# A two-layer hybrid trunk: layer 0's shift and scale loaded ahead of its gate, with scale and gate multiplied on VectorE

## What is computed

```python
def _rmsnorm(x, g):
    y = x * lax.rsqrt(jnp.mean(x * x, axis=-1, keepdims=True) + EPS)
    return y * g

# for each layer l, with c (latent) and c_ctx (context)
mod_x = silu(c) @ w_ada[l] + b_ada[l]          # 3 * 1024 columns
mod_c = silu(c_ctx) @ w_ada[l] + b_ada[l]
shift_x, scale_x, gate_x = split(mod_x, 3)     # the same for mod_c

hx = _rmsnorm(x, g_pre) * (1.0 + scale_x) + shift_x
hc = _rmsnorm(xc, g_pre) * (1.0 + scale_c) + shift_c
px, pc = hx @ w_in, hc @ w_in                  # all branches' inputs
...
total = sum(sigmoid(merge_i) * ((y_i * silu(z_i)) @ w_o[i]) for i in range(4))
x_new = x + gate_x * _rmsnorm(total @ w_out, g_post)
```

## Time and profile before

| | us |
|---|---|
| median of 3 runs | 2555.64 |
| lowest and highest | 2554.72, 2561.79 |
| profiled execution, its own time | 2555.41 |
| its span in the profile | 2553.4 |
| TensorE busy / DVE / ScalarE / GpSimd | 2465.6 / 1203.7 / 1091.7 / 1155.9 |

### The profile page before, as it was taken

How to read it: one execution, slowest core, us unless ns; L and a number is a source line. 1 busy time by engine, 2 the same in 40 slices (tenths; PEclk the granted TensorE clock), 3 DMA queues, 4 the chain that set the end, 5 groups by cost and what they waited for, 6 DMA issues and landing times.

```text
span 2553.4 us, 38113 instructions
## 1 busy us (share of the span) xinstructions
PE 2465.6 (97%) x12969; PEld 2082.7 (82%) x12969; DVE 1203.7 (47%) x1788; ACT 1091.7 (43%) x2287; POOL 1155.9 (45%) x948
## 2 busy tenths in 40 slices
PE   7897999999999999999999999999999999999998
PEld 1887988799888888888888788898888788888887
DVE  2453657496254466644243465781635333333322
ACT  2645564396212443344433443892214433343333
POOL 1576993123222355555555442222223555555553
PEclk9899999999999999999999999999999999999999
DMA  6355762100121155535333531001211333344333
GB/s 255 88 143 165 220 194 78 38 2 19 49 62 36 47 173 165 177 115 174 111 108 108 172 93 49 6 1 49 64 38 36 108 111 111 111 150 134 111 111 132
DMA packets 393275, 262.40 MB, mean 103 GB/s; under 512 B 16934, under 2 KB 365750, under 8 KB 391610
## 3 DMA queue, kind: packets, MB, share of 16 engines
q1 hardware_dynamic: 378944, 227.07, 29.8%
q10 hardware_dynamic: 14204, 33.67, 3.7%
HBM read 251.23 MB, written 9.45 MB: 102 GB/s over the span
## 4 chain that ended last, share of the span: by engine, by line
PE 83%; POOL 5%; DVE 5%; issue 4%; ACT 2%; DMA 1%; ACTq 0%; DVEq 0%; POOLq 0%; SPq 0%
PE ps L755 79%; POOL w_lo L651 4%; PE ps L947 2%; POOL w_lo L644 1%; DMA w_raw<-in_w_in 1%; DVE softmax_stats L2095 1%; DVE r_prev L2202 1%; PE ps L787 0%; DVE a_probT_lo L1837 0%; ACT w_hi L1287 0%; DMA w_ada<-in_w_ada 0%; ACT r_square L1287 0%; ACT a_prob L1463 0%; PE ps L887 0%; DVE a_out_sum L1837 0%
## 5 line engine op out<-in xcount | busy, mean ns | idle before, releaser
L644 POOL TENSOR_TENSOR w_lo<-w_raw,w_hi 128x512 fp32r<-128x512 f32 x596 | 811.1, 1365 | 1009.0 <-ACT w_hi L1287 1003.7
L755 PE MATMUL ps<-hT_hi,w_hi 128*128 128x512 f32 (+1 forms) x2528 | 940.9, 372 | 24.5 <-POOL w_lo L651 8.4
L755 PE MATMUL ps<-hT_hi,w_lo 128*128 128x512 f32 (+1 forms) x2528 | 929.6, 368 | 0.0
L755 PE MATMUL ps<-hT_lo,w_hi 128*128 128x512 f32 (+1 forms) x2528 | 929.0, 368 | 0.0
L1287 ACT ACTIVATE w_hi<-w_raw 128x512 fp32r<-128x512 f32 x712 | 445.2, 630 | 928.3 <-PE ps L755 855.0
L755 PEld LDWEIGHTS ps<-hT_hi,w_hi 128*128 128x128 f32 x2528 | 479.9, 190 | 111.3 <-issue 19.4
L755 PEld LDWEIGHTS ps<-hT_hi,w_lo 128*128 128x128 f32 x2528 | 479.6, 190 | 78.6
L755 PEld LDWEIGHTS ps<-hT_lo,w_hi 128*128 128x128 f32 x2528 | 480.2, 190 | 75.3
L1837 DVE TENSOR_TENSOR merge_tmp<-merge_tmp,ps 128x512 f32<-128x512 f32 (+1 forms) x160 | 101.5, 634 | 592.9 <-PE ps L755 434.2
L651 POOL TENSOR_TENSOR w_lo<-w_raw,w_hi 128x512 fp32r<-128x512 f32 x116 | 156.3, 1371 | 37.3 <-ACT w_hi L1287 36.9
L1837 DVE TENSOR_TENSOR merge_tmp<-merge_tmp 128x512 f32<-128x512 f32 (+1 forms) x120 | 166.9, 1390 | 4.1
(11 more groups left out here) (267 smaller groups left out, 3033.2 us busy)
## 6 DMA issues: line engine op xcount, KB each, us to landing
w_raw<-in_w_in SPq DMA_DIRECT2D x476, 256.0 KB, 2.9
w_raw<-in_w_o_rest SPq DMA_DIRECT2D x112, 256.0 KB, 2.8
w_raw<-in_w_out SPq DMA_DIRECT2D x74, 256.0 KB, 2.7
w_ada<-in_w_ada SPq DMA_DIRECT2D x8, 1536.0 KB, 9.3
ada_w<-in_w_ada SPq DMA_DIRECT2D x48, 256.0 KB, 3.3
w_raw_more<-in_w_in SPq DMA_DIRECT2D x72, 128.0 KB, 2.5
w_raw<-in_w_o_attn SPq DMA_DIRECT2D x32, 256.0 KB, 2.8
w_raw<-in_dft_x SPq DMA_DIRECT2D x16, 256.0 KB, 2.7
```

The costliest lines, as they stand in the source:

```text
L644: eng.tensor_tensor(w_lo[:, r, :], raw[:, r, :], w_hi[:, r, :].bitcast(F32), ALU.subtract).then_inc(sem["w_split"], tally.up("w_split"))
L755: return eng.matmul(dst, lhsT, rhs, start=start, stop=stop)
```

## The change

For layer 0 only:

- SP loads the small constants first, then only the first 2048 columns of w_ada (shift and scale, 8 slices of 128x2048, 1.05 MB each, up to three at a time), with the context's tokens behind the third slice, and only then the first weight units.
- TensorE multiplies three of the four 512-column groups. The fourth (the second half of scale) is summed on DVE, one product per slice and silu column with the partitions left unsummed (`scale_sums`). ScalarE copies the two sums to SBUF, and TensorE sums over the partitions with a row-selecting matrix (`add_rows`, two fp32 matmuls into bank 3).
- The gate's 1024 columns of w_ada are loaded in 16 pieces of 128x512 between the loads of the tiles F_Z and F_U of the context pass, into free columns of hT. DVE sums them in the first three sweeps of the context's merge (`gate_sums`, 32 instructions, 3 or 2 a step). In the fourth sweep ScalarE makes four copies, TensorE four fp32 matmuls and DVE the row. It is written at the fifth sweep's first step and read back, over 128 partitions, at the sixth's. ScalarE's wait for it ahead of the norm is gone.
- The norm's transposes go to banks 4, 5, 7 and 3, and the wait ahead of the first projection is gone.
- ScalarE splits the first three weight units behind the modulation instead of ahead of it.

```diff
+CTX_TURN = (4, 5, 7, 3)
...
             def modulation(p):
                 for k in range(KT):
-                    ada(p.layer, k)
+                    if k > 2:
+                        eng.wait_ge(ada_in[k - 3], 16)
+                    eng.dma_start(w_ada[k][:, :], a["w_ada"][p.layer][k * P:(k + 1) * P, 0:2 * D]).then_inc(ada_in[k], 16)
+                    if k == 2:
+                        for t in range(p.NT):
+                            eng.dma_start(token_tile(p, t), a["ctx"][0][t * P:(t + 1) * P, :]).then_inc(x_in[t], 16)
...
-                tiles(l, A_Q, 2)
                 if p.ctx:
+                    constants()
                     modulation(p)
-                tiles(l, A_Q + 2, F_U - 2)
+                tiles(l, A_Q, F_U)
                 tiles(l, F_Z, 2)
+                if p.ctx:
+                    gate_slices(p)
                 tiles(l, F_U, 2)
...
+            def add_rows(bank, first, second):
+
+                mm(ps[0:2, bank, :], sel[:, 1:3], first, True, False)
+                return mm(ps[0:2, bank, :], sel[:, 0:2], second, False, True)
...
-                    for n in range(6):
-                        ins = mm(ps[0:2, n, :], sT[:, :, k], w_ada[:, k, n * 512:(n + 1) * 512], k == 0, k == KT - 1)
+                    for n in range(3):
+                        ins = mm(ps[0:2, n, :], sT[:, :, k], w_ada[k][:, n * 512:(n + 1) * 512], k == 0, k == KT - 1)
...
+                        if p.opens and (i, j) == (3, 2):
+                            eng.wait_ge(sem["gate_copied"], tally.take("gate_copied"))
+                            for n in range(2):
+                                last = add_rows(4 + n, g_part[:, n, :], g_part[:, 2 + n, :])
+                            last.then_inc(sem["gate_rows"], tally.up("gate_rows"))
+                        if p.opens and (i, j) == (4, 0):
+                            eng.wait_ge(sem["gate_made"], tally.take("gate_made"))
...
                     norm(p)
                     pe_goes_on(eng, tally)
-                    eng.wait_ge(sem["hT_pre"], tally.now("hT_pre", 4))
                     project(p, 6, True)
...
-                eng.wait_ge(sem["gate_out"], tally.now("gate_out"))
...
-                for step in range(4):
+                scale_sums(0, 3)
+                scaled(p, 0)
+                scale_sums(3, 4)
+                eng.wait_ge(sem["small_in"], tally.take("small_in", 16 * 5))
+                for step in range(2):
                     log_gamma(step)
-                scaled(p, 0)
-                for n in range(6):
+                scale_sums(4, 5)
+                log_gamma(2)
+                scale_sums(5, 6)
+                log_gamma(3)
+                scale_sums(6, KT)
+                for n in range(4):
...
+            def times_silu(acc, w, s, k, name):
+
+                if k == 0:
+                    ins = eng.tensor_scalar(acc, w, sT[:, s, 0:1], None, ALU.mult)
+                else:
+                    ins = eng.scalar_tensor_tensor(acc, w, sT[:, s, k:k + 1], acc, ALU.mult, ALU.add)
...
+                        if p.opens and i < 3:
+                            q = 4 * i + j
+                            gate_sums(min(3 * q, 2 * q + 8), min(3 * q + 3, 2 * q + 10))
+                        if p.opens and (i, j) == (3, 3):
+                            gate_row_products()
```

More of the change, by code:

```diff
@@ L210, in trunk @@
         soft = const("softmax_stats", [P, 4, 4])
+        sel = const("row_select", [P, 3])
         rope = at("rope", [P, 2, SEQ], W + 14336)
@@ L215, in trunk @@
         turned = at("rope_turned", [P, SEQ], W + 12288)
-        w_ada = at("w_ada", [P, KT, 3 * D], 0)
-        m_rows = at("mod_rows", [P, 3 * D], W)
-        m_bias = at("mod_bias", [P, 3 * D], W + 3072)
-        m_gpost = at("mod_gpost", [P, D], W + 6144)
-        m_gate = at("mod_gate", [P, D], W + 7168)
+        w_ada = [at(f"w_ada{k}", [P, 2 * D], place) for k, place in enumerate(
+            (*(Z + 2048 * k for k in range(5)), W + 6144, W + 8192, W + 16384))]
+        w_gate = [at(f"w_ada_gate{n}", [P, KT, SEQ], 8192 * n)[:, :, 0:512] for n in range(2)]
+        g_part = at("gate_part", [P, 4, SEQ], 0)[:, :, 0:512]
+        m_rows = at("mod_rows", [P, 4, 512], W)
+        m_bias = at("mod_bias", [P, 2 * D], W + 3072)
+        m_part = at("mod_part", [P, 2, 512], W + 5120)
+        g_bias = at("gate_bias", [P, KT, SEQ], 0)[:, 0:4, 512:768]
+        g_post = at("gate_post", [P, KT, SEQ], 0)[:, 4:8, 512:768]
+        m_gate = at("mod_gate", [P, KT, SEQ], 8192)[:, 0:4, 512:768]
         n_stage = [at(f"ada_w{n}", [P, UNIT], Z + 1536 + 512 * n) for n in range(STAGED)]
@@ L1612, in rows_and_tables @@
                 def rows_and_tables():
-                    if not ada:
+                    if not ada and not p.opens:
                         gate_row()
@@ L1647, in body @@
                             log_gamma(j)
+                        if p.opens and i == 3 and j < 2:
+                            copy_gate_sums(j)
+                        if p.opens and (i, j) == (4, 0):
+                            save_gate(p.layer)
+                        if p.opens and (i, j) == (5, 0):
+                            eng.wait_ge(sem["gate_out"], tally.now("gate_out"))
+                            gate_row()
                         if latent and i == 1:
```

97 lines of the change are left out of this document (68 added, 29 removed).

## The result

The changed kernel takes **2537.35 us** (median of 3 runs, 2536.94 to 2537.40), against 2555.64 before: a ratio of 0.992, with a 95% interval of 0.9907 to 0.9934. That is 0.8% faster. The forecast was 2534, the range 2527 to 2546. The profiled execution has a span of 2535.3 us, 18.1 less than before; the sum had said 21.1 less. Run again beside the experiments it took 2535.55 us (5 runs, 2534.36 to 2538.51; span 2533.2), and the kernel before, 2557.17 (9 runs): 21.6 less, a ratio of 0.992 (0.9905 to 0.9932). Where an execution shows a low clock over its whole length (one of the four of n_banks_back, 4104.85 us at a mean granted clock of 0.56), it is left out of the medians.

A forecast was written before the change was run, and what follows sets the result against it. It took TensorE to bound the modulation at the start and GpSimd's weight split the context's merge; -20.6 - 1.9 + 0 - 1.3 + 2.1 + 0.6 = -21.1 from 2555.4 gave 2534 us, range 2527 to 2546.

The forecast's parts named there:

- Part 1: Start, shift and scale first: transposes of mod_rows start at 34.9 instead of 55.5 us, 20.6 us gained.
- DVE, not TensorE, is the last here: Start: DVE's sums end last, so the transposes start at 34.9 us; otherwise 33.3 or 32.2.
- rival 4: Start: DMA and TensorE alone bound the stage, transposes at 33.3 or 32.2, kernel 2532 to 2533 us; 17%.
- Part 2: Norm behind the start: ScalarE's missing wait and new banks bring the first projection sooner, 1.9 us gained (1.3 to 2.4).
- 1.1 us set aside for a low clock: First projection: 1.1 of 2.4 us gained is lost if its 12 matmuls run at 0.21 instead of 0.12 us.
- Part 3: Gate's 4.2 MB loaded between F_Z and F_U: some 2 us to spare, 0 lost, up to +5 if loads run slowly.
- Part 4: Context's merge: sums 0, gate row's load 1.3 gained, selecting matmuls 2.1 lost, finished row 0.6 lost.
- The gate row out of the burst: Merge: the gate row's 0.5 MB leaves the load burst at 222 us, 1.3 us gained.
- The selecting matmuls: Merge: four fp32 matmuls take TensorE 3.43 us, of which 2.1 us are lost (0 to 3.4).
- The gate row's products: Merge, end of fourth sweep: DVE makes the row, TensorE waits for it one step later; 0.6 us lost (0 to 2).
- Rivals 1 and 2: Merge sums take turns with the weight split, 2567 us, 4%; TensorE stays at 1.2 GHz at the start, 2553 us, 4%.
- Rival 3: F_U's first unit late, tokens late, or low clock on a fuller stage, +3 us each: 2537 to 2546 us; 20%.

The follow-up runs named there:

- n_banks_back: Changed kernel with the norm's turned tokens back in banks 0 to 3 and the first projection waiting for the last shift: 2537.84 us.

## Why the prediction was right, and where its sum was off

The mechanism, the sign and the range were right: the start carries nearly all of the gain, the sums are hidden in the merge, and the matmuls that select rows give some of it back. That the start's term came within 1.5 us is in part luck: putting DVE last made the gain 1.6 us smaller (34.9 instead of 33.3), and that hid half of the 3.1 us by which the late data moved the transposes (33.3 to 36.4). Point by point:

- **Part 1, the start: 19.1 instead of 20.6.** Two steps failed, one inside the other. "DVE, not TensorE, is the last here" is wrong: without most of its sums the stage ends at the same time (36.24). The order that rival 4 names, DMA and TensorE alone, is the real one. Its time (33.3 or 32.2) is not, because of the other step: "at 0.41 MB/us that is 23.0 us, and a load has about 2.2 us besides" counts from the first issue at full rate. The last slice lands at 30.8 instead of 28.1, since data flow only from 6.2 us on; the constants that the change moved onto SP's queue stand in front. I had listed which queues a moved load passes for the gate's slices, and not for ident, small and mask. With the delay removed the transposes start at 34.0, near the 33.3. TensorE's own work would hold the stage as long as the last slice does: its 48 passes take 23.2 us from 10.7 on, since the first six start 0.86 us apart and not 0.43. The prediction's 2.57 us a slice, 20.6 in all, leave that out. It reads the long first passes of the earlier trace rows as 1.2 GHz; the granted clock is 1.00 there in both traces, so no row shows that reading.
- **Part 2, the norm: 2.2 gained, 1.9 predicted.** The 1.1 us set aside for a low clock was not lost, since TensorE kept 2.4 GHz. A low clock wouldn't have cost it either: with the first slice in four requests the 12 matmuls ran at 1.2 GHz, and the distance was 8.56 us all the same. The banks are worth 1.7 us at that clock, at which the kernel before had run too, and ScalarE's missing wait the other 0.5 (10.74 against 10.27).
- **Part 3, the gate's loads: 0 predicted, no loss seen.** F_U's first unit did wait for its data (ScalarE idle 2.86 us before 164.13, and 2.23 in the second run), which the prediction had named as a sign of being wrong. So "2 us to spare" was too much, but the gain stands at 21.8 at the merge's first sigmoid, after 21.3 at the projection. It was not tested alone; the stretches at 1.2 GHz lie elsewhere in the two traces and may have covered or added some of it.
- **Part 4, the merge.** The gate row out of the burst: 0.9 (22.7 less 21.8), predicted 1.3. The sums: 0, as predicted. The selecting matmuls: 1.9, predicted 2.1. The gate row's products: 1.4, **predicted 0.6**, the term that was mis-sized. The prediction gives no working for its 0.6, only that TensorE waits for the row one step later. It sets the skill's rule beside it as a dearer case (1.2), and that case was the near one: 1.0 of the 1.4 comes from the product's two SBUF inputs. TensorE's wait did come (1.60 us); whether it or GpSimd's longer splits carry the cost is open, as they end within 0.2 us of each other. Net it is 1.9 + 1.4 - 0.9 = 2.4 lost, 1.4 predicted, and in the first trace a late weight unit (2.0) came on top, of which some later slack took a part: 3.0 from the first sigmoid on. In the second trace only 1.3 are lost from there to the fifth total, about the 1.4 of the sum, so the single prices add up to more than is seen together. No run takes away both the matmuls and the product.
- **Rivals 1 and 2** did not come: sums of 0.756 us, and a few passes above 592 ns. **Rival 3** describes what happened in size (2537.35 lies at its edge), but not in cause. Two of its events came and cost nothing that is seen: F_U's late unit, and the tokens, which ScalarE takes at 16.94 instead of 15.3 while DVE isn't last.

The 0.7 us between the eighth total and the end can't be told from the scatter: that stretch takes 2198.4 us before, and 2198.1 to 2200.3 in the thirteen traces of the changed kernel and its variants. What stays open: by which way the product's cost arrives, which of the three constants holds the first slice back, why the first slice in four requests came 0.6 us sooner, and why TensorE's clock fell near 39 us in two of these traces and not in the others.

## What to carry to other kernels

Ask of every load that a change moves, however small, what stands behind it in its queue: 194 KB of constants ahead of the first slice made it land 4.2 us later, while its 1.05 MB take 2.6 us at the full rate. Where GpSimd is the bound, a wait on another engine may be free (ScalarE's 2.19 us were) while a DVE instruction with both inputs in SBUF is not; feed it one operand from PSUM. Before a distance between two events is used as a measure, take it in traces that should not differ: one varied by 3 us here, another by 0.02. And before working out which of three engines is last, take away one engine's work and look whether the end moves.

## What the runs showed of the hardware

- With ident, small and mask ahead of it on the same queue, a 1 MB load asked for at 2.60 us landed at 10.59. With them on the other queue, one asked for at 1.19 landed at 6.35. From 4 to 6 us the DMA engines moved 45 GB/s (39 in the second run) and 341.
- A DVE product of 2x1024 took 2.26 us with both inputs in SBUF beside GpSimd's split and 1.21 with GpSimd idle; GpSimd's splits beside it took 1.94 us each. From PSUM, two of 2x512 took 1.28 us together, beside splits of 1.62.
- A DVE scaling of 128x1024 with one SBUF input took 0.75 us at the start, with GpSimd idle; the four in the merge, beside GpSimd's splits, took 1.33, 1.79, 1.76 and 0.73. A sum of 128x512 from SBUF onto PSUM took 0.756 beside the splits and 0.751 with GpSimd idle.
- In the bank experiment TensorE's granted clock fell to 1.2 GHz between 38 and 40 us, in the norm's transposes, and stayed there beyond 47; with the first slice in four requests it was 0.50 from 38 to 44. In the changed kernel, with the same work up to there, it stayed at 2.4 GHz in both traces. No run shows why.
